# Order of the first loads and of the weight rests in a sandwich-normed decoder trunk on one core

## The reference

```python
def _even_mixer(h, w_in, a_conv, b_conv, b_conv_bias, b_ln_g, b_ln_b, w_out):
    p = h @ w_in
    a_x, a_b, a_c, a_z, b_val, b_gate, b_z = jnp.split(p, 7, axis=-1)
    ya = a_b * _causal_dwconv(a_c * a_x, a_conv)
    yb = b_val * jax.nn.sigmoid(b_gate)
    yb = _causal_dwconv(yb, b_conv) + b_conv_bias
    yb = jax.nn.silu(_layernorm(yb, b_ln_g, b_ln_b))
    u = jnp.concatenate([ya * jax.nn.silu(a_z), yb * jax.nn.silu(b_z)], axis=-1)
    return u @ w_out
```

## Time and profile before

| | |
|---|---|
| median of 3 runs | 1347.03 us (1346.64 to 1347.7) |
| the profiled execution, its own time | 1346.3 us |
| its span, first to last instruction | 1344.5 us |
| TensorE busy | 1326.9 us, 99% of the span, 6054 matmuls |
| VectorE busy | 874.3 us, 65% |
| ScalarE busy | 440.7 us, 33% |
| GpSimd busy | 96.9 us, 7% |
| mean granted TensorE clock | 0.998 |
| DMA | 209.5 MB, mean 156 GB/s |

### The profile page before, as it was taken

How to read it: one execution, slowest core, us unless ns; L and a number is a source line. 1 busy time by engine, 2 the same in 40 slices (tenths; PEclk the granted TensorE clock), 3 DMA queues, 4 the chain that set the end, 5 groups by cost and what they waited for, 6 DMA issues and landing times.

```text
span 1344.5 us, 14691 instructions
## 1 busy us (share of the span) xinstructions
PE 1326.9 (99%) x6054; PEld 1104.8 (82%) x6054; DVE 874.3 (65%) x827; ACT 440.7 (33%) x436; POOL 96.9 (7%) x90
## 2 busy tenths in 40 slices
PE   8999999999999999999999899999999999999997
PEld 7888888888888888888888799888888888788886
DVE  6499999999846544536955984444522222499788
ACT  6421212221222121234555552222222223345452
POOL 0000000000009400000000100000000001400001
PEclk9999999999999999999999999999999999999999
DMA  9723333343368888753666554333343333364157
GB/s 319 218 63 94 102 106 105 94 125 94 102 179 274 250 258 250 251 188 107 241 258 233 163 161 125 96 95 95 100 113 94 94 94 95 125 219 157 43 208 251
DMA packets 229967, 209.50 MB, mean 156 GB/s; under 512 B 3616, under 2 KB 192160, under 8 KB 224928
## 3 DMA queue, kind: packets, MB, share of 16 engines
q1 hardware_dynamic: 225552, 203.61, 48.6%
q10 hardware_dynamic: 4368, 5.24, 1.2%
HBM read 187.87 MB, written 20.97 MB: 155 GB/s over the span
## 4 chain that ended last, share of the span: by engine, by line
PE 90%; DVE 5%; DMA 2%; ACT 1%; issue 1%; DVEq 0%; POOL 0%; SPq 0%; ACTq 0%
PE bank L705 30%; PE bank L709 30%; PE bank L707 30%; DVE w_lo L1490 1%; DMA scratch<-o_out 1%; DVE rows L1652 1%; ACT w_hi L1038 1%; DVE h_lo L1321 1%; DMA raw<-o_in 1%; DVE scratch L1522 1%; DVE rows L1569 0%; ACT junk L1190 0%; DVE scratch L1663 0%; DVE w_lo L1301 0%; DMA rows<-x_t 0%
## 5 line engine op out<-in xcount | busy, mean ns | idle before, releaser
L705 PE MATMUL bank<-h_hi,w_hi 128*128 128x512 f32 (+1 forms) x1536 | 585.6, 381 | 3.1 <-DVE w_lo L1343 1.6
L709 PE MATMUL bank<-h_hi,w_lo 128*128 128x512 f32 (+1 forms) x1536 | 584.0, 380 | 0.0
L707 PE MATMUL bank<-h_lo,w_hi 128*128 128x512 f32 (+1 forms) x1536 | 584.0, 380 | 0.0
L705 PEld LDWEIGHTS bank<-h_hi,w_hi 128*128 128x128 f32 x1536 | 288.8, 188 | 59.2 <-issue 4.0
L707 PEld LDWEIGHTS bank<-h_lo,w_hi 128*128 128x128 f32 x1536 | 288.8, 188 | 55.6 <-issue 0.7
L709 PEld LDWEIGHTS bank<-h_hi,w_lo 128*128 128x128 f32 x1536 | 288.8, 188 | 54.9
L1301 DVE TENSOR_TENSOR w_lo<-raw,w_hi 128x2048 fp32r<-128x2048 f32 x88 | 205.4, 2334 | 54.2 <-ACT w_hi L938 53.1
L1377 DVE SCALAR_TENSOR_TENSOR rows<-shifted,vecs,rows 128x512 f32<-128x512 f32 x256 | 198.8, 779 | 15.0 <-ACT rows L1000 7.6
L938 ACT ACTIVATE w_hi<-raw 128x2048 fp32r<-128x2048 f32 x88 | 167.9, 1910 | 87.3 <-PE bank L709 75.3
L705 PE MATMUL bank<-w_hi,h_hi 128*128 128x512 f32 x448 | 174.8, 390 | 0.6 <-DVE rows L1561 0.6
L709 PE MATMUL bank<-w_hi,h_lo 128*128 128x512 f32 x448 | 174.3, 389 | 0.0
(11 more groups left out here) (116 smaller groups left out, 718.3 us busy)
## 6 DMA issues: line engine op xcount, KB each, us to landing
raw<-e_in SPq DMA_DIRECT2D x52, 1024.0 KB, 5.7
raw<-o_in SPq DMA_DIRECT2D x32, 1024.0 KB, 6.1
scratch<-e_out SPq DMA_DIRECT2D x17, 1024.0 KB, 7.4
spare<-e_out SPq DMA_DIRECT2D x12, 1024.0 KB, 7.8
spare<-o_out SPq DMA_DIRECT2D x12, 1024.0 KB, 6.7
scratch<-o_out SPq DMA_DIRECT2D x10, 1024.0 KB, 5.1
e_sums<-scratch SPq DMA_DIRECT2D x8, 1024.0 KB, 5.1
spare<-e_sums SPq DMA_DIRECT2D x7, 1024.0 KB, 6.1
```

The costliest lines, as they stand in the source:

```text
L705: nc.tensor.matmul(dst, w[0], m[0], start=first, stop=False, skip_group_check=goes_on)
L707: nc.tensor.matmul(dst, w[0], m[1], start=False, stop=False, skip_group_check=goes_on)
L709: return nc.tensor.matmul(dst, w[1], m[0], start=False, stop=last, skip_group_check=goes_on)
```

## The change

It changes four things. (1) x tile 0 is a transfer of its own and SP's first; the first quarters of slabs 0 and 1 follow it, then x tile 1; `vecs` is issued by ScalarE's queue. Both engines treat the weights of the first quarter right after x tile 0. (2) ScalarE runs a one-column activation at the outset, once two constants are set, so that its table is loaded there. (3) Keep-warm is 8 matmuls rather than 12, and the spread matmul stands ahead of k = 8 of slab 4 rather than k = 4. (4) In channel tiles 0 and 1 VectorE makes rests of weights earlier: in tile 0 that of slab 7 after tap 10; in tile 1 that of slab 9 ahead of tap 1, of slab 10 after tap 10, of slab 11 after tap 20. ScalarE makes the high part of slabs 7 and 11 ahead of its wait for bank `first + 3`.

```diff
-            def load_x(pair):
-                at = slice(2 * pair, 2 * pair + 2)
+            def load_x(at, loaded):
                 sp.dma_start(rows[:, at, :], x_t.rearrange("(k p) t -> p k t", p=P)[:, at, :])\
-                    .then_inc(x_loaded[pair], 16)
+                    .then_inc(loaded, 16)
+
+            def load_x_pair(pair):
+                load_x(slice(2 * pair, 2 * pair + 2), x_loaded[pair])
...
-            sp.dma_start(vecs[:, :], vec).then_inc(vec_loaded, 16)
+            load_x(slice(0, 1), x_first_loaded)
             for j in range(4):
-                load_x(2 * j)
+                if j > 0:
+                    load_x_pair(2 * j)
                 for n in range(RAW):
                     load_first(n, j)
-                load_x(2 * j + 1)
+                if j == 0:
+                    load_x(slice(1, 2), x_loaded[0])
+                load_x_pair(2 * j + 1)
...
-            keep_warm(12)
+            keep_warm(8)
...
-                if (q, k) == (0, QUARTER):
+                if (q, k) == (0, 2 * QUARTER):
...
             act.sem_inc(hi_ready, SLOTS)
+            act.dma_start(vecs[:, :], vec).then_inc(vec_loaded, 16)
+            act.wait_ge(consts_set, 2)
+            nc.scalar.activation(junk[:, 0, 0:1], minus_half[:, :], ACT.Identity, bias=0.0,
+                                 scale=1.0)
...
-                    if k % 2 == 0:
+                    if k == 0:
+                        act.wait_ge(x_first_loaded, 16)
+                    elif k == 1 or k % 2 == 0:
                         act.wait_ge(x_loaded[k // 2], 16)
                     x_rounded(k)
-                    if k % 4 == 1:
+                    if k % 4 == (0 if j == 0 else 1):
                         for q in range(RAW):
                             first_split(q, j)
...
                 if c > 0:
                     split_ahead(c, 2)
                     split_ahead(c, 3)
+                if c < 2:
+                    split_ahead(c + 1, 0)
                 act.wait_ge(bank_free[first + 3], first_used(c))
                 nc.scalar.activation(tile(c), prod[:, PAD - CONV_A + 1:PAD - CONV_A + 1 + T],
                                      ACT.Identity, bias=0.0,
                                      scale=tap("conv_a", c, CONV_A, 0)).then_inc(seeded_a, 1)
-                split_ahead(c + 1, 0)
+                if c >= 2:
+                    split_ahead(c + 1, 0)
...
                 dve.wait_ge(seeded_b, c + 1)
+                if c == 1:
+                    split_ahead(c, 2)
                 convolve(c, conv_done, glu, CONV_B, "conv_b", 1, 11)
-                if c > 0:
+                if c == 0:
+                    split_ahead(c + 1, 0)
+                elif c == 1:
+                    split_ahead(c, 3)
+                else:
                     split_ahead(c, 2)
                 convolve(c, conv_done, glu, CONV_B, "conv_b", 11, 21)
-                if c > 0:
+                if c == 1:
+                    split_ahead(c + 1, 0)
+                elif c > 1:
                     split_ahead(c, 3)
...
                 convolve(c, conv_done, glu, CONV_B, "conv_b", 23, 25)
-                split_ahead(c + 1, 0)
+                if c > 1:
+                    split_ahead(c + 1, 0)
```

More of the change, by code:

```diff
@@ L197, in build @@
         e_sums = nc.dram_tensor("e_sums", [3, 4, P, SLAB], F32, kind="Internal").ap()
+        x_first_loaded = sem("x_first_loaded")
         x_loaded = [sem(f"x_loaded{p}") for p in range(KT // 2)]
```

## The result

The changed kernel takes 1352.47 us (median of 9 runs, 1350.51 to 1353.73), the kernel before 1347.70 us in the runs beside it. The ratio is 1.0035, 95% interval [1.0026, 1.0043]: 4.7 us slower, 3.5 to 5.8. The predicted time was 1350.7 us, 1.8 us less; 0.7 of these are the kernel before itself, whose median was 1347.03 us when the forecast was made and 1347.70 us in the runs beside this one. The profiled execution of the changed kernel took 1352.47 us, its span is 1350.7 us against 1344.5.

A forecast was written before the change was run, and what follows sets the result against it. The prediction took TensorE's matmul stream to bound the kernel up to 731 us. Start -2.1, slab 10 +4.5 and clock +1.3 made +3.7 on the 1347.03 us median: 1350.7 us, range 1348.3 to 1352.7.

The forecast's parts named there:

- The start: First product near 6.4 us; k = 2 waits for x tile 2 and begins at 10.1 instead of 12.24: gain 2.1 us.
- The price behind the landing: From pair 1's landing to k = 2: 0.05, rounding to rest 0.83, the rest 0.75, then 0.15 us.
- Keep-warm hidden: Ahead of the first product: the 16 passes left end near 6.3 us, just before it, so they cost nothing.
- The spread and the copy: Slab 4: spread matmul at k = 8, 56.5 us, without stall; VectorE's copy of it at 57.55, 0.62 us later than before.
- VectorE's floor: Earliest start of VectorE's copy of the spread matmul, where VectorE came free: 56.51 us.
- Rests and the read of bank 2: Tile 1: VectorE's weight rests delay its bank 2 read to 121.61 us, so slab 10 begins 2.4 us later than before.
- Later slacks: After slab 10: VectorE ends tile 1 as before, TensorE is 2.4 us later, so slacks grow; no later wait absorbs the delay.
- The clock at slab 10: TensorE's 4.3 us pause there drops the granted clock to 0.50, costing 1.3 us.
- The middle between the bounds: Cost of a mid-kernel clock fall: between nothing and 2.55 us, taken as 1.3.
- The sum +3.7: Whole kernel: -2.1 us at the start, +4.5 at slab 10, +1.3 of clock.

The follow-up runs named there:

- start only: The change without its part 4 (weight rests in their old order), against the kernel before: 1348.47 us, +0.3 us.
- matmuls in the pause: The change plus 16 unused small matmuls ahead of TensorE's wait at slab 10: 1349.81 us, +2.3 us against the kernel before.
- table late: The change with bank 2 read ahead of tap 1, without the early activation loading ScalarE's table: 1346.17 us, -2.2 us against the kernel before.
- keep-warm 12: The change with bank 2 read ahead of tap 1, 12 keep-warm matmuls instead of 8: 1346.53 us, -0.7 us against the kernel before.
- the pair whole: The change with bank 2 read ahead of tap 1, x tiles 0 and 1 in one transfer, weights behind tile 1: 1347.22 us; with 12 keep-warm matmuls 1347.13.

## Why the prediction was right

By its own steps:

- **The start: 2.1 us predicted, 1.6 in the profiled execution.** That the stream is held by a landing and not by the first product, which came 2.8 us earlier, was right. Which landing was right only in part: in the profiled execution TensorE waited last for x tile 1, now a transfer of its own, which the sum has no term for, and found x tile 2 ready. The two lie close: by the same rule as below, an estimate, pair 1 alone would have allowed 1.7 us. Of the eight traces with the first tile by itself and the short keep-warm, x tile 1 is the last to hold the stream in three (the change, start only, matmuls in the pause), pair 1 in five. The size was off because these transfers landed late, pair 1 at 8.9 instead of 8.3 and x tile 1 by 7.6.
- **The price behind the landing: 1.8 us, about right.** That 10.7 less 8.9 is 1.8 is no proof of it, since k = 2 didn't wait in this trace. Where it did, it began 1.6 us behind the landing (9.1 to 10.7 in "table late"), and another 0.2 went by before the stream was dense. Over the nine traces whose first tile comes by itself pair 1 landed between 8.2 and 9.6, and the gain moved between 2.2 and 1.0 with it; apart from keep-warm 12 it is always 10.6 less that landing, within 0.1. The landing was behind 8.5, that of before, in seven of the eight traces with the short keep-warm. The Trainium skill (Trainium Kernel Development and Optimization, Key Constraints) says that all queues run on the same 16 DMA engines and interleave. That spoke for 8.5 where the sum took 8.3, and the traces agree as far as they go; no run puts `vecs` back on SP's queue alone.
- **Keep-warm hidden: right for this change, by a narrow margin.** It ended at 6.3 and the first product came at 6.7. In the traces of the kernel with the pair whole, the same eight passes are worth 1.6 us; the times of these two kernels don't show it.
- **The spread and the copy: 57.55 predicted, 58.05.** The 0.5 us are those that the start lacks. VectorE's floor, 56.51 before, was 57.9 here, because the token squares came 1.4 us later (their transfers landed later): it bound just as closely, and the prediction had it 1 us away.
- **Rests and the read of bank 2: right.** ScalarE's rounding held VectorE by 1.84 us (2.79 - 0.95; 1.81 predicted), the extra rest took 2.21, and the read ended at 122.17 (121.61 predicted). Slab 10 began 3.0 us late (2.4 predicted), the difference being the copy's. TensorE waited 4.4 us.
- **Later slacks: right as far as 735 us.** The stream is 4.68 us late there as at 130 us. What came behind was not in the forecast: 0.3 us at the first transposes, and 1.1 us for a second fall of the clock at the old pause near 770 us. The prediction took the earlier trace rows to say that a pause of 2.3 us is harmless. It is not; the profiled execution of before was one without a fall.
- **The clock at slab 10: 1.3 predicted, 1.69.** It fell 5.3 us after the last matmul, 0.9 us after TensorE had gone on, stayed at 0.50 (1.2 GHz) for 3.41 us, and matmuls took 0.427 us instead of 0.227: 8 of them by 0.2 us. The middle between the bounds was low; the estimate from the Trainium skill (TensorE: Matmul & The Clock Gate, HAM oscillation), 0.8 us, was lower still. What that section says, that each wait of 3 to 5 us re-throttled TensorE, agrees with the one idle stretch of that length here, 4.4 us. It has no example of the shorter ones: at slab 10 the clock fell at all three pauses of 2.2 to 2.7 us too, and near 770 us in seven of the twelve traces that have the pause of 2.3 us.

The sum +3.7 is short by 1.0 us of the measured 4.7. In the profiled execution 0.6 of it is missing at slab 10 and 0.4 in the clock, and the stream is 4.68 us late there. That this is the measured 4.7 once more is in part luck: at the end the two profiled executions are 6.2 us apart, and the medians contain executions with and without a fall near 770 us on either side.

Open: how often the clock falls at slab 10 in executions that were not profiled, and so how the 4.7 us divide into pause and clock on average. Every execution has a mean granted clock, and one low stretch of 3.41 us takes 0.0013 from it (3.41 x 0.5 / 1345). The nine executions of the change have 0.997 (three, 1350.5 to 1351.6 us), 0.996 (two) and 0.995 or 0.994 (four, 1352.5 to 1353.7 us). That fits at least one fall in most of them, but the means are rounded to 0.001, and the low stretch behind the last matmul differs by about 3 us between the traces. "Matmuls in the pause" against the change says 2.4 us for the clock, with intervals of over 1 us on either side. Why the first landings vary by 1.4 us between executions was not tried.

## What to carry to other kernels

Work that is pulled forward on an engine's list pushes back all that it passes: look in that list for reads that free a buffer or bank, since their slack doesn't show as a wait in the profile before (here 1.1 us against 2.8 us added). Often such a read can stand at the front itself, where its input is long ready; one instruction of 0.7 us moved turned +4.7 us into -1.8.

A head start is worth what the next late thing leaves of it: here the first product came 2.8 us sooner and the stream 1.6, by the landings of the transfers behind the first. And a pause of the matmul engine of a few us can cost its length and then some, by the clock behind it; where it couldn't be removed here, matmuls without use in it kept the clock.

## What the runs showed of the hardware that was not expected

- A pause of 2.2 to 2.7 us in the middle of dense matmuls can drop the granted clock, and doesn't always: at the same place, near 770 us, it fell in seven traces out of twelve, at slab 10 in three out of three. The shorter pauses inside the work, 1.5 us and less, left it alone in every trace. The fall may come after the matmuls have gone on (0.9 us after, at slab 10). Each of the low stretches inside the work lasted 3.41 us in the traces, and those behind a pause at slab 10 or near 770 us cost 1.0 to 1.7 us.
- The same pause near 770 us may explain much of the spread of the kernel before, whose times gather near 1346.3 and near 1348; no execution of it with a fall was profiled. Its 98 executions beside the experiments fit this: the 41 with a mean granted clock of 0.998 or more have a median of 1346.7 us, the 57 below that of 1348.3 us.
- The shorter keep-warm left 2.0 us idle ahead of the first product in the kernel with the pair whole, and its matmuls went at the low rate until 11.8 us; with keep-warm to 8.0 us the clock was up at 8.2, before the first product. With the table late, 1.7 us idle did no such harm, since the clock had come up before them.
